# Which chunk stands outside the ring of weights at four stage borders, and who adds the final output

## The reference, cut to what matters

```python
for l in range(2):
    y = swiglu_2(rms_norm(x, ffn1_pre_g[l]), ...);   x = x + 0.5 * rms_norm(y, ffn1_post_g[l])
    y = hybrid_mixer(rms_norm(x, mix_pre_g[l]), ...);  x = x + rms_norm(y, mix_post_g[l])
    y = memory_xattn(rms_norm(x, xa_pre_g[l]), ...);   x = x + rms_norm(y, xa_post_g[l])
    y = swiglu_2(rms_norm(x, ffn2_pre_g[l]), ...);   x = x + 0.5 * rms_norm(y, ffn2_post_g[l])
```

## Time and profile before

| | us |
|---|---|
| median of 3 runs (3340.97 to 3342.39) | 3341.98 |
| the profiled execution, its time | 3337.08 |
| the profiled execution, its span | 3335.4 |
| TensorE busy with products | 3256.0 |
| vector engine, ACT, GpSimd busy | 1285.2, 1238.0, 1337.1 |

### The profile page before, as it was taken

One profiled execution on the slowest core, in us unless ns is written; L12 is line 12 of the kernel. 1 busy time (PEld: TensorE's weight loads), 2 busy tenths in 40 slices (PEclk: granted clock), 3 DMA queues, 4 the chain that ended last, 5 costly groups with the idle time before them and its releaser, 6 DMA issues.

```text
span 3335.4 us, 45757 instructions
## 1 busy us (share of the span) xinstructions
PE 3256.0 (98%) x17988; PEld 2764.8 (83%) x17988; DVE 1285.2 (39%) x2527; ACT 1238.0 (37%) x2301; POOL 1337.1 (40%) x861
## 2 busy tenths in 40 slices
PE   8999999999999999999999999999999999999998
PEld 6886788888888988888688889888987888788887
DVE  5465343205330424644353304431144564354311
ACT  4454332223322344554433223322344554343321
POOL 3452344453444442344334443444442244144442
PEclk9999999999999999999999999999999999999999
DMA  3221223231233241122222232232331122123231
GB/s 141 76 76 44 65 95 100 92 125 62 92 98 102 80 133 58 52 83 83 70 70 94 93 104 83 96 100 95 108 127 51 39 86 93 38 83 101 96 99 66
DMA packets 81236, 287.32 MB, mean 86 GB/s; under 512 B 8960, under 2 KB 11392, under 8 KB 80640
## 3 DMA queue, kind: packets, MB, share of 16 engines
q1 hardware_dynamic: 79584, 278.42, 25.6%
q10 hardware_dynamic: 1440, 5.98, 0.5%
HBM read 282.26 MB, written 2.10 MB: 85 GB/s over the span
## 4 chain that ended last, share of the span: by engine, by line
PE 88%; DVE 5%; ACT 2%; POOL 2%; issue 2%; DMA 1%; ACTq 0%; DVEq 0%; POOLq 0%
PE bank L264 22%; PE bank L266 22%; PE bank L265 22%; PE bank L272 4%; PE bank L273 4%; PE bank L274 4%; PE bank L1284 3%; POOL wlo L258 2%; PE bank L1260 2%; PE bank L1271 2%; PE bank L3024 1%; ACT whi L244 1%; DMA raw<-wstream 1%; PE bank L649 1%; DVE m_xbc L1877 1%
## 5 line engine op out<-in xcount | busy, mean ns | idle before, releaser
L258 POOL TENSOR_TENSOR wlo<-raw,whi 128x256 fp32r<-128x256 f32 (+2 forms) x778 | 1221.7, 1585 | 1663.3 <-ACT whi L244 1619.5
L264 PE MATMUL bank<-hhi,whi 128*128 128x512 f32 x2160 | 863.0, 400 | 9.9 <-POOL wlo L258 5.3
L265 PE MATMUL bank<-hlo,whi 128*128 128x512 f32 x2190 | 855.9, 391 | 0.0
L266 PE MATMUL bank<-hhi,wlo 128*128 128x512 f32 x2160 | 845.6, 391 | 0.0
L244 ACT ACTIVATE whi<-raw 128x1024 fp32r<-128x1024 f32 x504 | 503.1, 1033 | 355.6 <-PE bank L266 290.3
L264 PEld LDWEIGHTS bank<-hhi,whi 128*128 128x128 f32 x2160 | 408.0, 189 | 94.3 <-issue 13.3
L265 PEld LDWEIGHTS bank<-hlo,whi 128*128 128x128 f32 x2190 | 413.8, 189 | 81.6 <-issue 1.0
L266 PEld LDWEIGHTS bank<-hhi,wlo 128*128 128x128 f32 x2160 | 407.3, 189 | 87.1
L264 PE MATMUL bank<-ff_ahi,whi 128*128 128x512 f32 x660 | 256.7, 389 | 0.0
L266 PE MATMUL bank<-ff_ahi,wlo 128*128 128x512 f32 x660 | 256.7, 389 | 0.0
L265 PE MATMUL bank<-ff_alo,whi 128*128 128x512 f32 x630 | 245.1, 389 | 0.0
(11 more groups left out here) (405 smaller groups left out, 5691.5 us busy)
## 6 DMA issues: line engine op xcount, KB each, us to landing
raw<-wstream SPq DMA_DIRECT2D x516, 512.0 KB, 3.7
raw<-wstream SPq DMA_DIRECT2D x20, 256.0 KB, 3.1
x<-xT ACTq DMA_DIRECT2D x4, 512.0 KB, 10.3
xa_v<-memT ACTq DMA_DIRECT2D x2, 1024.0 KB, 4.9
outT<-x SPq DMA_DIRECT2D x4, 512.0 KB, 2.8
consts<-consts ACTq DMA_DIRECT2D x1, 1062.0 KB, 15.4
m_lw<-lru_w ACTq DMA_DIRECT2D x1, 544.0 KB, 3.6
par<-par SPq DMA_DIRECT2D x2, 248.0 KB, 11.4
```

The costliest lines, as they stand in the source:

```text
L258: last = g.tensor_tensor(h.lo[:, o:o + step], h.raw[:, o:o + step], h.hi[:, o:o + step].bitcast(F32), ALU.subtract)
L264: t.matmul(out, l[0], r[0], start=start, stop=False)
L265: t.matmul(out, l[0], r[1], start=False, stop=False)
L266: return t.matmul(out, l[1], r[0], start=False, stop=stop)
```

## The change

The last chunk of the projection (O3) and the first of the next stage (F0) stand outside the ring, where F0 and F1 did. This holds behind the second mixers and the memory attention; behind a feed-forward stage `Entry` still places F0 and F1. ACT's order becomes: evacuation of O0, high parts of O2 and of O3, evacuation of O1, high parts of F0 and of F1, evacuation of O2, high parts of F2. GpSimd's order of low parts stays.

At the exit the gains are multiplied by 0.5 once (a new operation of 128x8), so the additions have no factor any more. GpSimd does six of the first half's additions and two of the second's. The vector engine does the first half's eight scalings in a row, the second half's mean, two additions of the first half, and then the second half with six additions. SP waits for the marks of both engines.

```diff
 class Entry:
-        places = stage.spare()
-        k.elsewhere[self.first], k.elsewhere[self.first + 1] = places[0:2], places[2:4]
         self.third_made = isinstance(stage, FeedForward)
+        if self.third_made:
+            places = stage.spare()
+            k.elsewhere[self.first], k.elsewhere[self.first + 1] = places[0:2], places[2:4]
 class Exit:
+    POOLS = (6, 2)
+        self.gains, self.gains_made = k.stat[:, 144:144 + KT], k.marks("out_gains", 1)
+    def pool_add(self, n, half):
+        g, (y, x) = self.k.nc.gpsimd, self.parts(n, half)
+        g.wait_ge(*self.scaled[KT * half + n])
+        g.tensor_tensor(x, y, x, ALU.add).then_inc(self.pool_added[half].sem)
     def pool(self):
-        for half in range(2):
-            self.before[half].pool()
+        self.before[0].pool()
+        for n in range(4):
+            self.pool_add(n, 0)
+        self.before[1].pool()
+        for n in range(4, self.POOLS[0]):
+            self.pool_add(n, 0)
+        for n in range(self.POOLS[1]):
+            self.pool_add(n, 1)
+    def dve_scale(self, n, half):
+        v, (y, x) = self.k.nc.vector, self.parts(n, half)
+        if n == KT - 2:
+            v.wait_ge(*self.sums.kept[6 + half])
+        v.scalar_tensor_tensor(y, y, self.gains[:, n:n + 1], self.before[half].row(), ALU.mult, ALU.mult).then_inc(self.scaled.sem)
+    def dve_add(self, n, half):
+        v, (y, x) = self.k.nc.vector, self.parts(n, half)
+        v.wait_ge(*self.scaled[KT * half + n])
+        v.tensor_tensor(x, y, x, ALU.add).then_inc(self.dve_added[half].sem)
     def dve(self):
+        v.tensor_scalar(self.gains, self.gain(0, KT), self.factor, None, ALU.mult).then_inc(self.gains_made.sem)
         self.before[0].dve()
...
+        v.wait_ge(*self.gains_made[0])
+        v.wait_ge(*self.before[0].rows[0])
+        for n in range(KT):
+            self.dve_scale(n, 0)
+        self.before[1].dve()
+        for n in range(self.POOLS[0], KT):
+            self.dve_add(n, 0)
+        v.wait_ge(*self.before[1].rows[0])
+        for n in range(KT + 1):
+            if n < KT:
+                self.dve_scale(n, 1)
+            if n > self.POOLS[1]:
+                self.dve_add(n - 1, 1)
 class OutProj:
     def act(self, made=0):
-        end = len(self.chunks)
+        end, early = len(self.chunks), self.nk <= KT
...
-            if not (self.by_half and n == end - 2):
+            if not self.by_half or n < end - 3 or n == end - 3 and not early:
                 weight_hi(self.k, ch.c + 2, 1 if n == 0 and made else None)
-            if self.by_half and n == end - 3:
+            if self.by_half and (n == end - 3 or n == 0 and early):
                 weight_hi(self.k, ch.c + 3)
 class MixerTwo and class MemoryAttention, ahead of their OutProj:
+        last, places = len(k.chunks) + 3, self.spare()
+        k.elsewhere[last], k.elsewhere[last + 1] = places[0:2], places[2:4]
 sp_program:
-        s.wait_ge(*m.out.added[4 * n + 3])
+        if n == 1 or n == 2:
+            s.wait_ge(*m.out.added(m.out.POOLS[half] - 1, half))
+        s.wait_ge(*m.out.added(n % 2 * 4 + 3, half))
```

More of the change, by code:

```diff
@@ L951, in __init__, with added, parts @@
         self.before = sums.roots = [HalfRoot(k, sums, half, (row_bank, sums.b)[half]) for half in range(2)]
-        self.scaled, self.added = k.marks("y_scaled", 2 * KT), k.marks("x_added", 2 * KT)
+        self.gains, self.gains_made = k.stat[:, 144:144 + KT], k.marks("out_gains", 1)
+        self.scaled = k.marks("y_scaled", 2 * KT)
+        self.pool_added = [k.marks("out_pool_added", n) for n in self.POOLS]
+        self.dve_added = [k.marks("out_dve_added", KT - n) for n in self.POOLS]
+    def added(self, n, half):
+        first = self.POOLS[half]
+        return self.pool_added[half][n] if n < first else self.dve_added[half][n - first]
+    def parts(self, n, half):
+        o = slice(n * T + half * TH, n * T + (half + 1) * TH)
+        return self.sums.y[:, o], self.k.x[:, o]
     def pe(self):
@@ L966, in dve @@
     def dve(self):
-        k, v, sums = self.k, self.k.nc.vector, self.sums
+        v = self.k.nc.vector
+        v.tensor_scalar(self.gains, self.gain(0, KT), self.factor, None, ALU.mult).then_inc(self.gains_made.sem)
         self.before[0].dve()
[L969 to L983, removed]
+        v.wait_ge(*self.gains_made[0])
@@ L3149, in __init__ @@
             f = stage(FeedForward(k, e, False, y))
-        self.out = stage(Exit(k, f.sums, p2("ffn2_post_g"), 0.5, 5))
+        self.out = stage(Exit(k, f.sums, lambda n, w: k.p2(LAYERS - 1, "ffn2_post_g", n, w), 0.5, 5))
         assert len(k.chunks) == k.n_chunks, (len(k.chunks), k.n_chunks)
```

## The result

| | before | after |
|---|---|---|
| median, first comparison (4 and 4 runs) | 3342.18 | 3321.68 |
| lowest to highest | 3340.97 to 3344.44 | 3320.02 to 3324.26 |
| profiled execution, its time | 3337.08 | 3323.15 |
| its span | 3335.4 | 3321.8 |

The ratio is 0.995, with a 95% interval of 0.9938 to 0.9962: 13 to 21 us faster, 20.5 between the medians. I had forecast 10.9 us and 3331.1, with a range from 3328.8.

A forecast was written before the change was run, and what follows sets the result against it. TensorE, with 88% of the chain, was taken to bound the kernel; four gaps at its column sums (8.4 us) plus the exit (2.5) gave 10.9 us off the 3341.98 median, 3331.1, range 3328.8 to 3336.8.

The forecast's parts named there:

- The ring part: Output projections of second mixer and memory attention: moving O3 outside the ring brings O2's squares in time, saving 8.4 us.
- The gaps: TensorE idles 1.83 to 1.88 us ahead of L649's column sums, once in each of four four-chunk output projections.
- F1's ring place: Next stage's start: F3's high part must wait for F1's release; forecast to cost nothing, up to 8 us covered.
- the mixer's cover: Mixer borders: spare time between the end of both additions of squares and TensorE's need, 1.1 us at worst.
- Rival A: Additions of squares stay late in the mixers, so half the ring gain is lost: 6.7 us, 3335.3; chance 0.12.
- The exit part: Last scalings and additions: GpSimd takes eight additions, gaining 2.5 us; bounds 0 and 3.0.
- newly open wait: Exit: vector engine idles 0.9 us before the second row, a wait that was covered before.
- Taken: 4 x 2.11 = 8.4 us: Four gaps ahead of L649, each priced at 2.11 us by product-start spacing, drain included; bounds 0 and 8.5.
- the same difference off the median: Profiled execution lies 4.9 us below the median; this was carried over unchanged: 3341.98 - 10.9 = 3331.1.
- B: Exit gives nothing, as every meeting of vector engine and GpSimd is paid: 8.4 us, 3333.6; chance 0.08.
- C: TensorE waits at the point after L649's sums instead; only the exit's 2.5 us gained, 3339.5; chance 0.07 with another rival.
- D: F1's late release delays ACT's row and the next stage's products: net 8.7 us slower, 3350.7; chance 0.03.

The follow-up runs named there:

- x1_ring: Only the chunk places and ACT's new order, exit as before, against the kernel before: ratio 0.9964, 12 us faster.
- x5_gap_short: Changed kernel plus one unused 4096-column reduction ahead of the last addition of squares at four borders: 0.9983 of before, 11.3 us above the changed kernel.
- x4_order: Kernel before with one edit: ACT makes F1's high parts behind O2's evacuation, places as before; ratio 0.9971 of before, 9.7 us faster.
- x7_pool4: Changed kernel with four instead of two of the second half's exit additions on GpSimd: 0.9946 of before, median 3321.1 against 3321.2.
- x2_exit: Only the exit change, places and ACT's order as before, against the kernel before: ratio 0.9991, 3.0 us faster.

## Why the prediction was wrong

**The ring part's mechanism was right, at all four borders.** The gaps are gone, each gives back 2.11 us by the spacing, 8.4 together, and F1's ring place costs nothing. Span times clock says 7.8 +-0.5 for x1_ring. My replay put the mixer's cover at 1.1 us and it is 0.3: there the pair of additions ends at 2799.27, since the pair took 5.73 us, where I had counted 5.1 for the slowest (the same pair had taken 5.25 us in the mixer before). Rival A was nearer than I made it, but did not come.

**The exit part was right in mechanism and size:** 2.4 us by the trace, 2.5 forecast, with one meeting of two engines and the newly open wait of 1.19 us (forecast 0.9).

**The step that failed is "Taken: 4 x 2.11 = 8.4 us"**, with its upper bound, "8.5 if all goes". It priced a gap by its idle time and its drain, from one execution in which none of the four gaps was followed by a low clock. In others it is: 8.5 us in the 12 gaps of the three traces with the gaps of before, so 2.8 us for one execution of that kernel. The five traces without these gaps have no such stretch at any of their 20 borders, and x5_gap_short, which puts the gaps back, has one again and 5.0 +-1.7 us more of low clock. By the executions' own clocks the gaps cost more than the traces say: the low clock's share is 4.6 +-1.5 us smaller in x1_ring and 6 us smaller in x4_order, against 28.8 for the kernel before (mean of its 54 executions). The traces and the clocks agree that it is not nothing, and are too few to say whether it is 3 or 6. So the step failed by leaving this term at nothing; as the price of the gaps at the full clock 8.4 us stands (7.8 +-0.5 measured).

**The second half of the same error is the sentence "the same difference off the median".** The profiled execution lay 4.9 us below the median. I carried that along as a constant. Part of it was a sign that the ordinary execution has more low-clock stretches than this one: its own low-clock share is 26.9 us, against 28.8 in the mean of 54. That explains 1.9 us, and 3338.9, the mean of the 54, is just that much above 3337.1. The other 3 us lie in the first executions of before, which were all between 3341.0 and 3344.4; their clocks are not on record, so this can be chance but is not shown. What the change removes is also what makes some of these stretches, so even the explained part could not be expected to stay. Taken off 3338.9, the forecast would have been 3328.0, still 6 us above the 3322.0 of the changed kernel. After the change it has indeed turned: the profiled execution lies 1.5 us above the median.

**The account.** The whole change gives 17.0 us between the means of all executions (54 of before at 3338.9, 10 of after at 3322.0): 10.9 as forecast, of which the full-clock time shows 9, since half of what is saved in the idle exit counts as low clock; and some 6 us of fewer low-clock stretches. The 20.5 of the first comparison holds 3 to 4 us more; the changed kernel has the same median there as later (3321.7 and 3321.2) and the kernel before has not (3342.2, later 3337.8 and 3338.4), so that remainder lies in the four executions of before. Whether it is chance or something in that measurement is not shown. Of the 13.6 us between the two profiled spans, 10.9 are the forecast's; the other 2.7 are a little less than two stretches at half clock of 1.7 us loss each, which the execution of before had in the attention stages (near 1616 and near 2575) and that of after had not; such stretches come and go there in all kernels.

**Rivals.** B, C and D did not come: one of eight GpSimd additions meets the vector engine, L649's next wait is not there, and F3's wait costs nothing. The rule of the Trainium skill that I weighed (SBUF — State Buffer, section Who interferes with whom) is agreed with by the addition of 0.68 us at 3315.10, which starts while GpSimd's last operation runs until 3315.50. In x7_pool4, where GpSimd runs on, two additions take 0.55 and 0.58; an addition that meets nothing takes 0.41, so they were held for 0.14 and 0.17 us, the rest of a GpSimd operation of 0.7 us that was under way. No rival of mine spoke of the clock: I had thought only of ways in which less is gained, and left 2.3 us below the forecast for a gain beyond it. The chances were also added up wrongly: by the split given there faster has 0.84 and same 0.13, not 0.82 and 0.15.

**What stays open.** Why one gap of 1.9 us is followed by a stretch at half clock and the next is not. The Trainium skill (TensorE: Matmul & The Clock Gate, section Part 1: The HAM clock gate) says that what steers the gate runs freely and is not reset when a kernel starts, so that the point at which the clock changes varies from run to run. This case's traces agree in so far as the same four gaps were followed by three such stretches in one execution and by none in another; what decides it in one case they do not show. Open is also the exit's share of the low clock (x2_exit has 25.8 +-0.6 there against 28.8, where a shorter idle end explains 1.2), and in the ring part the 2 to 3 us between what the clocks and what the traces say.

## What to carry to other kernels

A gap on TensorE costs more than its idle time: price it with its drain, from start to start of the products around it, and, where the clock can fall behind it, with the stretch at half clock that follows in part of the executions. When the profiled execution is faster than the median, ask which stretches it lacks and whether the change touches what causes them, before carrying the difference over. Two fixes that remove the same wait need not be worth the same; follow the engine that is made later by each (here GpSimd) to its next duty.

## What the runs showed of the hardware that I had not expected

Ahead of the sums of L649, gaps of 1.8 to 2.1 us on an otherwise busy TensorE were followed by 3.4 to 7 us at 1.2 GHz in 5 of 14 cases, and gaps of 0.84 us in none of 2; gaps of 5.2 to 6.1 us in 4 of 4, all in one execution, with the fall inside the gap and about 10 us of work at half clock behind it. The length of one gap does not decide it. In the memory attention's own products TensorE waits 1.1, 0.3 and 0.5 us within 2 us (lines 3010 and 3024), and in the ten traces 12 of these 20 places have 3.4 us at half clock there (here in the first trace of the kernel before, ahead of the stretch of 3 us in which the clock is 0.50):

```profile
1613.47 0.44 PE L3010 MATMUL bank<-consts,xa_s 128*128 128x128 f32 x2 [1.13 <-DVE xa_s L3089]
1614.19 0.44 PE L3010 MATMUL bank<-consts,xa_s 128*128 128x128 f32 x2 [0.28 <-DVE xa_s L3089]
1615.10 2.17 PE L3024 MATMUL bank<-xa_p,xa_v 128*128 128x512 f32 x3 [0.47 <-ACT xa_p L3054]
...
1616.00:1619.00 3.00, 3.00 (x5) 1.23 (x4) 0.22 (x1) 0.60 (x1) 0.00 (x0) 0.50 0.00 0
```

Neither the change nor any run touches these waits. Twenty-four executions of one kernel spread over 16 us, almost all of it in the granted clock (0.989 to 0.994).
